# A gated delta rule inside a two-block model: preparation, inverses and factors rearranged

## What is computed

```python
qkv = silu(dwconv(dn_qkv, conv_dn))          # 5 taps over positions
q = l2norm(q) * 128 ** -0.5; k = l2norm(k)   # rsqrt(sum(x * x) + EPS) per head
beta = sigmoid(...); g = -exp(a_log) * softplus(...)
# in a chunk, with G = cumsum(g), decay_ij = exp(G_i - G_j) for i >= j
A = I + strictly_lower(beta * (k @ k.T) * decay)
u, w = solve(A, [v * beta, k * beta * exp(G)])
attn = (q @ k.T) * decay
v_new = u - w @ state
o = (q * exp(G)) @ state + attn @ v_new
state = state * exp(G_last) + (k * exp(G_last - G)).T @ v_new
```

## Time and profile before

| | |
|---|---|
| time, 3 runs | 1908.32 us median (1905.60 to 1911.94) |
| profiled execution | 1907.14 us, span 1905.3 us |
| busy: PE, DVE, ACT, POOL | 86%, 57%, 39%, 6% of the span |
| mean granted TensorE clock | 0.901 of full speed |
| read from HBM | 250 MB, 132 GB/s over the span |

### The profile page before, as it was taken

The page is one execution under the profiler, slowest core; times in us unless marked ns, Lnnn a source line. Parts: engine busy times, 40 slices in busy tenths (PEclk is TensorE's granted clock), DMA queues, the critical chain, the costliest instruction groups (busy, mean ns, idle before and its releaser), DMA issues. The chain is left out here.

```text
span 1905.3 us, 35594 instructions
## 1 busy us (share of the span) xinstructions
PE 1642.4 (86%) x14964; PEld 1554.9 (82%) x14964; DVE 1091.5 (57%) x1639; ACT 738.5 (39%) x994; POOL 114.4 (6%) x139
## 2 busy tenths in 40 slices
PE   3999989858899988999886887779998989679997
PEld 2999979837888988999885775679997875579997
DVE  6994458868785465444465653554434446654434
ACT  2444346630005534553345000346433434346532
POOL 0121000002220000110000210000000020000000
PEclk7999999859999999999988995789999995589999
DMA  8895534303132353454341000234443430125451
GB/s 335 316 346 189 188 136 167 120 0 100 58 127 98 133 177 133 178 189 169 127 165 45 2 2 7 89 109 170 156 164 111 155 117 1 45 90 194 159 181 63
DMA packets 36992, 252.86 MB, mean 133 GB/s; under 512 B 4099, under 2 KB 5508, under 8 KB 7684
## 3 DMA queue, kind: packets, MB, share of 16 engines
q1 hardware_dynamic: 36436, 248.97, 36.6%
q10 hardware_dynamic: 432, 2.10, 0.3%
HBM read 250.00 MB, written 1.05 MB: 132 GB/s over the span
## 5 line engine op out<-in xcount | busy, mean ns | idle before, releaser
L430 DVE TENSOR_TENSOR w_lo<-raw,w_hi 128x2048 fp32r<-128x2048 f32 (+2 forms) x203 | 456.4, 2250 | 537.3 <-ACT w_hi L422 536.8
L496 PE MATMUL bank<-x_hi,w_hi 128*128 128x256 f32 (+1 forms) x2224 | 648.1, 291 | 64.5 <-DVE x_lo L645 38.7
L497 PE MATMUL bank<-x_lo,w_hi 128*128 128x256 f32 (+1 forms) x2224 | 640.3, 288 | 0.0
L498 PE MATMUL bank<-x_hi,w_lo 128*128 128x256 f32 (+1 forms) x2224 | 639.8, 288 | 0.0
L422 ACT ACTIVATE w_hi<-raw 128x2048 fp32r<-128x2048 f32 (+2 forms) x203 | 381.6, 1880 | 458.9 <-PE bank L498 423.1
L496 PEld LDWEIGHTS bank<-x_hi,w_hi 128*128 128x128 f32 x2224 | 429.2, 193 | 73.3 <-issue 65.2
L498 PEld LDWEIGHTS bank<-x_hi,w_lo 128*128 128x128 f32 x2224 | 430.9, 194 | 0.0
L497 PEld LDWEIGHTS bank<-x_lo,w_hi 128*128 128x128 f32 x2224 | 429.3, 193 | 0.9 <-issue 0.7
L496 PE MATMUL bank<-mh_hi,w_hi 128*128 128x272 f32 (+1 forms) x512 | 148.6, 290 | 6.5 <-PEq L2029 6.5
L498 PE MATMUL bank<-mh_hi,w_lo 128*128 128x272 f32 (+1 forms) x512 | 147.5, 288 | 0.0
L497 PE MATMUL bank<-mh_lo,w_hi 128*128 128x272 f32 (+1 forms) x512 | 147.2, 287 | 0.0
(11 more groups left out here) (425 smaller groups left out, 2162.5 us busy)
## 6 DMA issues: line engine op xcount, KB each, us to landing
raw<-in_stream SPq DMA_DIRECT2D x227, 1024.0 KB, 4.8
raw<-in_stream SPq DMA_DIRECT2D x8, 768.0 KB, 4.2
raw<-in_stream SPq DMA_DIRECT2D x4, 512.0 KB, 3.2
h<-in_h ACTq DMA_DIRECT2D x1, 1088.0 KB, 5.8
out<-h SPq DMA_DIRECT2D x8, 128.0 KB, 1.9
cst<-in_const ACTq DMA_DIRECT2D x1, 896.0 KB, 10.0
turning<-in_turning SPq DMA_DIRECT2D x1, 336.0 KB, 2.8
pool_w<-in_pool_w SPq DMA_DIRECT2D x1, 288.0 KB, 2.7
```

Of the source, the lines that this page charges most:

```text
L430: nc.vector.tensor_tensor(w_lo[:, s_at % 2, 0:kt], raw[:, r_at % RING, 0:kt], w_hi[:, s_at % 2, 0:kt].bitcast(F32), ALU.subtract).then_inc ...
L496: nc.tensor.matmul(out, hi, xh[:, k0 + k, 0:L], start=start, stop=False)
L497: nc.tensor.matmul(out, hi, xl[:, k0 + k, 0:L], start=False, stop=False)
L498: mm = nc.tensor.matmul(out, lo, xh[:, k0 + k, 0:L], start=False, stop=stop)
```

## The change

- **Modulation slabs** leave the inverses: 22 run beside all of the first up-projection (`up1`), 2 beside `ca_b`, 10 beside the first ten pairs of the second up-projection (`up2a`).
- **Beta and decays** are computed after `ca_b` (PE's 32 columns), the softplus series is cut into pieces between the slabs of `ca_c` and `ca_v`.
- **qkv** is unrolled flat over 12 pairs in the order k, v, q. DVE keeps two taps (4 instructions); POOL computes the two others and adds (4 tensor_scalar of 256 columns, 2 additions of 512 per pair). PE gets work between slabs: cumulated decays, sums of squares of k as 16 matmuls of one column, 32 transposes, decay rows of direction 0, k-k products. ACT copies rows out, scaling v by the inverse of k's factor, and takes the exponents of direction 0 after slab 10.
- **Length norms**: k is not scaled; its factor enters `beta_k`, v's rows and later terms as a per-row scalar. q's length leaves altogether: `q_sq` is added, on POOL, to the squares in the head norm of the last stage.
- **Inverses** (`Inverse`) grow only to 64-blocks, over 6 levels, in tiles of 64 columns; matmuls have 64 rows, 64 columns of weights and 32 moving columns, one for each diagonal 64-block. The off-diagonal block follows from two more products; ACT writes all into `whole_t`. The RWKV chunks use the same class.
- **Direction 1's preparation** is handed in beside `apply(0, ...)`; k-q products of direction 0 stand beside levels 1 to 4 of the first inverse.
- **Storage**: `attn_t`, `whole_t`, `q_exp1` and `k_end` lie over `w_hi` and `w_lo`, so the first slab of `gates0` is split only at the start of the last mixer stage.

The diff, cut to its core:

```diff
-    add("up1a", BESIDE_UP, by_halves("w_ffn1_up"), between=ada_order[UPFRONT:UPFRONT + BESIDE_UP], rs=2)
-    add("up1b", FF1T - BESIDE_UP, by_halves("w_ffn1_up", BESIDE_UP))
+    add("up1", FF1T, by_halves("w_ffn1_up"), between=ada_order[UPFRONT:UPFRONT + BESIDE_UP], rs=2, ada0=UPFRONT)
     add("down1", 4, by_cols("w_ffn1_down", [8, 8, 6]), [8, 8, 6])
-    add("ca_b", 2, w_in(0), taker="act")
+    add("ca_b", 2, w_in(0), between=ada_order[UPFRONT + BESIDE_UP:ADA_LATE], rs=2, taker="act")
     add("ca_c", 2, w_in(CA), taker="act")
     add("ca_v", 2, w_in(2 * CA))
-    add("qkv", 12, w_in(3 * CA), taker="act")
+    add("qkv", 12, by_parts("w_in", [3 * CA + QK, 3 * CA + 2 * QK, 3 * CA]), taker="act", flat=True, cut=True)
...
+    add("up2a", late, by_halves("w_ffn2_up"), between=ada_order[ADA_LATE:], rs=2, ada0=ADA_LATE)
...
+                def product(bank, done, left, right):
+                    for k in range(nh):
+                        for rows in self.quads:
+                            mm = nc.tensor.matmul(bank[rows, k * half:(k + 1) * half], left(rows, k), right(rows, k), start=True, stop=True)
+                    mm.then_inc(done, 1)
+                for l in range(self.levels):
...
+                    for c in range(2):
+                        pe.wait_ge(y_done, a0["y"] + 2 * l + c + 1)
+                        product(banks[c], p_ready, lambda rows, k: self.a_t[rows, c, k, rows], part(self.x, c, self.source))
+                    if between:
+                        between(l)
+                    for c in range(2):
+                        pe.wait_ge(p_done, a0["p"] + 2 * l + c + 1)
+                        if l:
+                            product(banks[2 + c], xu_ready, lambda rows, k: self.y[rows, c, k, 0:self.W], part(self.prod, c, self.source))
+                        product(banks[4 + c], yu_ready, lambda rows, k: self.prod[rows, c, k, 0:self.W], part(self.y, c, self.target))
+                if len(self.quads) == 2:
...
+                    for c in range(2):
+                        pe.wait_ge(y_done, a0["y"] + n + c + 1)
+                        for k in range(nh):
+                            mm = nc.tensor.matmul(banks[c][o, k * QUAD:(k + 1) * QUAD], self.a_t[e, c, k, o], self.x[e, c, k], start=True, stop=True)
+                        mm.then_inc(p_ready, 1)
...
+                def exponents():
+
+                    for q in range(4):
+                        c, hh = quarter(q)
+                        act.wait_ge(gb_taken, q + 1)
+                        nc.scalar.activation(dec_0[:, c, hh:hh + 4], dec_0[:, c, hh:hh + 4], ACT.Exp).then_inc(dec_exp, 1)
...
+                    if n:
+                        silu(n - 1)
+                    if n >= 2:
+                        rows_out(n - 2)
...
+                    if n == 10:
+                        exponents()
...
+            @block.gpsimd
+            def _(pool):
+                for n in range(12):
+                    b = n % 2
+                    pool.wait_ge(tap_done, n + 1)
+                    for k in range(4):
+                        tap, j = 3 + k // 2, k % 2
+                        ins = nc.gpsimd.tensor_scalar(late[:, tap - 3, j], win[:, b, j, tap:tap + T1], conv_w(n, tap, j), None, ALU.mult)
+                    ins.then_inc(conv_pool, 1)
+                    pool.wait_ge(conv_pool, 2 * n + 1)
+                    nc.gpsimd.tensor_tensor(late[:, 0], late[:, 0], late[:, 1], ALU.add).then_inc(conv_pool, 1)
+                    pool.wait_ge(conv_pool, 2 * n + 2)
+                    pool.wait_ge(conv_dve, n + 1)
+                    nc.gpsimd.tensor_tensor(wsum[:, b], wsum[:, b], late[:, 0], ALU.add).then_inc(conv_done, 1)
...
+                    if n == 11:
+                        dve.wait_ge(end_exp, 1)
+                        nc.vector.tensor_scalar(g_exp[:], g_exp[:], -1.0, None, ALU.mult)
+                        for q in range(4):
+                            scaled_gram(dve, 0, q, dec_0, GRAM_0[q], 0)
...
+                    m = n - 2
+                    if m in KEYS:
+                        pe.wait_ge(k_squared, m + 1)
+                        for c in range(2):
+                            for j in range(2):
+                                at0 = 320 + 8 * c + 2 * m + j
+                                mm = nc.tensor.matmul(banks[6][:, at0:at0 + 1], k_sq[:, m % 2, j, c * P:(c + 1) * P], const("ones")[:, 0:1], start=True, stop=True)
+                        mm.then_inc(ss_ready, 1)
...
+                        decay_rows(pe, 0, q, banks[7])
+                    if n == 10:
...
+                        for q in range(4):
+                            key_gram(pe, q, GRAM_0[q])
...
+        in_hi, in_lo = (nc.alloc_sbuf_tensor_at(f"over_w{n}", [P, 2 * SLAB], F32, offset=w_at + n * 2 * SLAB * 4) for n in range(2))
+        attn_t = [in_hi[:, n * 2 * D:(n + 1) * 2 * D].rearrange("p (c h n) -> p c h n", c=2, h=HEADS) for n in range(2)]
...
+                        for q in ((0,), (1,), (2, 3))[n - 2]:
+                            if q:
+                                pe.wait_ge(a_done, 4 + q)
+                                pe.wait_ge(attn_done, 4 + q)
+                            key_gram(pe, q, banks[6])
+                            query_gram(1, q, banks[7])
+                inverse[0].on_pe(pe, beside_first)
+                apply(0, beside_apply)
+                inverse[1].on_pe(pe)
+                apply(1, lambda n: None)
...
+                split_hi(act, (S["gates0"], 0, numbers(S["gates0"], None, 0, 0, 0)))
```

More of the change, by code:

```diff
@@ new lines, in decay_exponent, with key_gram @@
+        def decay_exponent(dve, d, q, dec, bank, base):
+            c, hh = quarter(q)
+            dve.wait_ge(gb_ready, base + q + 1)
+            for k in range(4):
+                ins = nc.vector.scalar_tensor_tensor(
+                    out=dec[:, c, hh + k], in0=bank[:, k * P:(k + 1) * P], scalar=g_cum[:, d, c, hh + k:hh + k + 1],
+                    in1=const(("neg_upto", "neg_from")[d]), op0=ALU.subtract, op1=ALU.add)
+            ins.then_inc(gb_taken, 1)
+        def key_gram(pe, q, bank):
+            c, hh = quarter(q)
+            for k in range(4):
+                kt = qkv[:, HEADS + hh + k, c * P:(c + 1) * P]
+                mm = nc.tensor.matmul(bank[:, k * P:(k + 1) * P], kt, kt, start=True, stop=True)
+            mm.then_inc(gram_ready, 1)
@@ L989, in _, with last_modulation @@
+                        ins = nc.vector.scalar_tensor_tensor(out=wsum[:, b, j], in0=win[:, b, j, tap:tap + T1], scalar=conv_w(n, tap, j),
+                                                             in1=wsum[:, b, j], op0=ALU.mult, op1=ALU.add)
+                        if k != 2:
+                            ins.then_inc(conv_step if k < 2 else conv_dve, 1)
+                dve_pairs(dve, sec, taps, beside)
             @block.tensor
             def _(pe):
-                for name in ("ca_b", "ca_c", "ca_v", "qkv"):
-                    pe_pairs(pe, S[name], x_hi, x_lo, T1, norm=norm_mix if name == "ca_b" else None)
+                def last_modulation(i, u, U):
+                    if u == 1:
+                        pe_ada(pe, S["ca_b"].r0 + 3, ADA_IN_MIX, ADA_IN_MIX % 2)
@@ new lines, in solved, with apply @@
+                def solved(first, half, c):
+                    for k in range(4 * half, 4 * half + 4):
+                        mm = nc.tensor.matmul(banks[half][:, (k % 4) * P:(k % 4 + 1) * P], whole_t[:, c, k], (v_rows if c == first else v_new)[:, c, k], start=True, stop=True)
+                    mm.then_inc(z_ready, 1)
+                def apply(d, beside):
+                    first, second, H = d, 1 - d, 2 * d
+                    inverse[d].wait_whole(pe)
+                    for half in range(2):
+                        solved(first, half, first)
+                    beside(0)
@@ L1297, in _ @@
+                    for half in range(2):
+                        for k in range(4 * half, 4 * half + 4):
+                            mm = nc.tensor.matmul(banks[2 + half][:, (k % 4) * P:(k % 4 + 1) * P], v_new[:, first, k], attn_t[d][:, first, k], start=True, stop=True)
+                        mm.then_inc(o_ready, 1)
+                    beside(2)
                     for half in range(2):
                         pe.wait_ge(r_done, H + half + 1)
-                        for k in range(4 * half, 4 * half + 4):
-                            mm = nc.tensor.matmul(banks[half][:, (k % 4) * P:(k % 4 + 1) * P], inv_t[:, second, k], v_new[:, second, k], start=True, stop=True)
@@ new lines, in decays @@
+                def decays(q):
+                    c, hh = quarter(q)
+                    act.wait_ge(gb_taken, 4 + q + 1)
+                    nc.scalar.activation(dec_1[:, c, hh:hh + 4], dec_1[:, c, hh:hh + 4], ACT.Exp).then_inc(dec_exp, 1)
+                ends(0)
+                inverse[0].on_act(act)
+                query_factors(0)
+                query_factors(1)
+                states(0)
+                for q in range(4):
```

(22 more changed lines are left out.)

836 lines of the change are left out of this document (470 added, 366 removed).

## The result

The kernel after takes 1961.53 us (median of 4 runs, 1958.66 to 1965.98), the kernel before in the same session 1906.96 (1902.67 to 1911.94): ratio 1.0287, 95% interval 1.0255 to 1.032. It is slower by 54.6 us. The profiled execution of the kernel after has a span of 1956.9 us at a mean granted clock of 0.857 (before: 1905.3 at 0.901).

What follows compares the result with a forecast made beforehand. PE was taken to bound the qkv projections and the application, a chain of small steps between engines the stage after the projections. Terms summed to -47.1 us, from 1907.1 to 1860, range 1816 to 1895.

Steps and rivals of the forecast that it cites:

- first inverse: First mixer inverse: passes alternating between two places cost 29.4 ns, 44.4 us with query products against 52.1, -7.7 us.
- Modulation slabs: Both feed-forwards: each pair that gets a slab costs 0.36 us, +2.2 us in the first and +3.6 in the second.
- Projections ca: Around `ca_b` and `ca_c`: PE's moved matmuls, DVE's modulation and split, and the wait behind ACT cost +10.4 us.
- Within qkv: Beside qkv projections: PE's 144 passes cost +17 us, table loads and first pairs +3; POOL's 5.4 us per pair hides.
- After the last slab: From the last qkv matmul to the inverse: 75.1 us shrink to a tail of 9.3, -65.8 us.
- Rival D: Removed chain is paid elsewhere: PE's 23 us, a 15 us tail, stalls of 25; 1891 us, chance 0.12 shared with Rival B.
- Application 0: Application of direction 0 with direction 1's preparation beside it: 30 us against 27.6, +2.4, PE waiting for two banks.
- Last mixer stage: Start of the last mixer stage: the first slab's split by ACT and DVE now precedes the first matmul, +4.4 us.
- RWKV: RWKV's chunks: -2.2 us for each inverse of 128, +0.7 for the chunk of 16, sum -3.7 us.
- Rival A: Inverses: diagonal tiles writing one bank don't overlap, passes cost 53 to 56 ns, +84 us, 1944 us; chance 0.09.
- Rival B: Beside qkv: POOL is the bound at 9.0 us per pair against 6.9, 1885 us; chance 0.12 shared with Rival D.
- Rival C: Inverses: a pass costs by its moving columns, 15 ns, some 16 us less per direction, 1818 us; chance 0.10.

Runs made afterwards that it cites:

- e1: The kernel after, with each pass of the inverses' levels moving all 64 columns instead of 32: 1874.36 us, ratio to before 0.9844.
- d1: The kernel after, with 64 moved columns in the first three levels of the inverses and 32 from the fourth on: 1870.65 us (one run).
- w1: The kernel after, with eight unused 128x128 matmuls ahead of each of the first stage's two inverses: 1899.74 us (one run).
- p1: The kernel after, with all eight taps of a qkv pair on DVE and no POOL work beside the projections: 1944.31 us, ratio 1.0202.
- a1: e1 with each product's passes reordered, all heads of one 64-block and then all of the other: 2015.58 us (one run).
- b1: e1 with p1's edit, so 64 moved columns and all eight taps on DVE: 1859.05 us, ratio 0.9753.
- f1: The kernel after, with 64 moved columns in the first level of the inverses alone and 32 from the second on: 1875.26 us (one run).
- w2: The kernel of w1 again, unchanged, timed in ten runs: 1897.44 us, ratio to before 0.9957.
- e2: The kernel after, 32 columns kept, with four unused 128x128 matmuls in front of each product of an inverse of 128: 2200.15 us (one run).
- z1: b1 with unused matmuls where PE waits: six before each inverse of 128, 16 and 6 in RWKV's preparation: 1857.19 us, ratio 0.9737.

## Why the prediction was wrong

The step that failed is the price of a pass in the *first inverse*: "The new tiles keep 64 columns of weights and alternate between two places: 29.4 ns again." The places did alternate and the price at the full clock was right to 0.3 ns (e1, d1, w1). What was carried over unsaid was the clock of 0.93. The working allowed for "level 0 at a slow clock", and then for a rise as in the kernel before. The passes of 32 moved columns didn't raise it: that overlooked condition, and not the overlap of the tiles, is what failed. At 0.50 a pass costs 53.3 ns, and this term failed three times: by the last two columns it cost 29.7 us in the first inverse, 27.9 in the second and 27.2 in RWKV's chunks, 84.8 of the 98.7 us between forecast and result.

Point by point, against the table:

- *Modulation slabs*, +2.2 and +3.6 forecast: the mixer starts 1.6 us later, and the stretch that holds the second ten slabs is 1.1 us longer. Slightly overpriced, the more so as that stretch begins, behind PE's pause of 5.46 us, at a low clock that the sum left out as well (0.59 over its first 5.8 us with 31 matmuls, before 1.00 with 49).
- *Projections ca*, +10.4: with the first +2.2 it came to +14.9 instead of +12.6. DVE waited 12.1 us for ACT's exponents, in front of the second slab of `ca_c`.
- *Within qkv*, +17 and +3 in the sum: +31.5. This is the second failed term. POOL's 5.4 us a pair was 8.4; the upper bound of 9.0 had been taken from an addition beside a busy DVE, and was the better row; the multiplications took 0.92 us at least, as the two-input row (0.91), where 0.6 was taken. p1 gave 17.2 us back. Its stretch from the `ca` product to the last matmul is 92.4 us, 17.8 more than before, by PE's 144 passes (17 forecast).
- *After the last slab*, -65.8: -65.5. The removed chain was a chain, and all of it was won. Rival D's tail of 15 us is out (9.6); stalls beside the slabs of the size that it named did come, through POOL.
- *Application 0*, +2.4: +0.7, and -0.7 in e1. PE's waits for the two banks at its end exist, but are short (1.00 and 1.08 us).
- *Second inverse*, -12.9: +11.9; in e1, -16.0.
- *Last mixer stage*, +4.4: +6.7 with slow passes in front, +4.3 in e1.
- *RWKV*, -3.7: +28.6; in e1 +1.5. From copies to copies e1's second chunk did win (44.9 us for 50.3), but the products ahead of the first inverse, which the change doesn't touch, ran at 0.50 there and at a full clock before, and cost 5.6 us (18.5 us from the first product to the copies, 12.9 before).
- *Rival A* had the right size (1944, for 1961.5) and the wrong place. Its mechanism is refuted: tiles of one bank overlapped in the kernel after itself (30 passes in 0.89 us), in e1, and by the contrast with a1. The rule of the Trainium skill that was weighed there (TensorEngine Tiling (Array Packing), section Gotcha 1: PSUM Pressure) is that different row tiles can't access one bank at once. As the prediction read it, passes of the two tiles would follow one another; they started 29 ns apart, and the measurement decides.
- *Rival B* held, with 17 us.
- *Rival C* is out: at the full clock 32 and 64 columns cost the same. That agrees with the floor of about 25 ns from start to start in the Trainium skill (TensorE: Matmul & The Clock Gate, section Wait — 56ns, not 53.3ns?); measured were 29.1.

With both causes repaired (b1) the total is the forecast: 1859 measured, 1860 forecast. It is luck in good part. b1 leaves POOL out, where the forecast had a POOL that hides, and its stages miss in both directions. Too dear were the `qkv` slabs with the tail by 5.6 us (98.3 from the `ca` product to the copies, 103.9 forecast), application 0 and the second inverse by 3.1 each and the second feed-forward by 1.2. Too cheap were RWKV by 9.2, what follows it by 1.8, the last mixer stage by 1.5, the first inverse by 1.1 and `ca` by 0.6.

The case was visible in advance. The earlier trace rows showed 0.65 and 0.93 in neighbouring stages, passes of small tiles at 0.50. A rival "the tiles are light, the clock stays at 0.50" would have followed, at the price of A.

## What to carry to other kernels

When passes get smaller, carry the clock as a term of its own: a full PE in the profile is no sign of a full clock, and the same passes cost 29 or 53 ns a piece. Before giving up on small tiles look at the stage's clock and at the pause in front; moving more columns than wanted in one level, or a few unused dense matmuls in a pause, was worth 86 us (f1, one run) and 64 us (w2) here. Check the clock in the trace afterwards: e2 shows that dense passes alone don't settle it. An idle POOL is not free beside a DVE that reads two tensors: price it by a row taken under that load.

## What the runs showed of the hardware

- Of two kernels that differ in 32 or 64 moved columns, the one that moves twice as many was 87 us faster, by the clock alone.
- Within an inverse of small passes alone the clock kept the level that it had after the first products. At 0.50 the levels of 32 columns ran for 50 us with PE busy without pause and didn't rise (432 to 482 us); at 1.00 the same levels didn't fall (d1, f1, w1). A pause of 1.66 us in front, followed by passes of 32 columns, let it fall; the same pause followed by passes of 64 didn't (e1, f1); followed by eight dense passes and then passes of 32 it did (e2). Behind the levels a pause of 0.7 us was enough in w1's first inverse (the next 16 passes took 3.4 us, in e1 2.05), f1, b1 and z1, and not in e1. What decides these runs don't settle: a1 moves 64 columns and stayed at 0.50 in the first stage but rose in RWKV, e2's stream ran at both, and b1 and e1 differ over the same instructions.
- The Trainium skill (TensorE: Matmul & The Clock Gate, Part 1) puts the clock down to how busy the PE has been, with a rise after sustained activity. Here the trace agrees for e1's tiles; with those of the kernel after, 50 us of unbroken passes brought no rise.
- Two diagonal 64x64 tiles in turn cost 54 ns a pass at 0.50 and 29 at 1.00; one place alone 95 at 0.50 and 60 at 1.00 (cross-block products). Runs of 16 passes in one place and then 16 in the other cost 84 at 0.50 (a1).
- POOL's multiplication of 256 columns took 0.92 us at least and 1.40 on average under load, more per column than its addition of two tensors (1.27 for 512), and DVE's two-tensor instruction of 0.48 took 1.5 beside such an addition.
